# Modulation vectors turned in pairs by transposes, an early first split, and a factor applied after the last output tile of mixer two

## What is computed

```python
mod = (silu(c) @ w_ada[l] + b_ada[l])          # 6 x 1024
shift_m, scale_m, gate_m, shift_f, scale_f, gate_f = split(mod, 6)
h = rms_norm(x, norm_mix[l]) * (1 + scale_m) + shift_m
x = x + gate_m * hybrid_mixer(h, ...)          # stick-breaking heads and gated linear attention
h = rms_norm(x, norm_ffn[l]) * (1 + scale_f) + shift_f
x = x + gate_f * hierarchical_moe(h, ...)      # 32 experts
...
# layers of the second kind
mix = concat([rms_norm(y_a, g_a), y_b, rms_norm(y_c, g_c), rms_norm(y_d, g_d)])
x = x + mix @ w_out[l]
x = x + square(relu(rms_norm(x, g) @ w_up[l])) @ w_down[l]
```

## Time and profile before

| | us |
|---|---|
| median of three runs | 1703.4 (1702.81 to 1707.79) |
| profiled execution, its own time | 1698.64 |
| its span | 1696.8 |
| TensorE busy | 1616.9 |
| VectorE busy | 1175.3 |
| ScalarE busy | 927.8 |

### The profile page before, as it was taken

The page is one execution under the profiler, slowest core; times in us unless marked ns, Lnnn a source line. Parts: engine busy times, 40 slices in busy tenths (PEclk is TensorE's granted clock), DMA queues, the critical chain, the costliest instruction groups (busy, mean ns, idle before and its releaser), DMA issues.

```text
span 1696.8 us, 24960 instructions
## 1 busy us (share of the span) xinstructions
PE 1616.9 (95%) x10392; PEld 1385.3 (82%) x10392; DVE 1175.3 (69%) x1380; ACT 927.8 (55%) x1192; POOL 99.1 (6%) x68
## 2 busy tenths in 40 slices
PE   6999989999999999899999998998999999989997
PEld 3676779999996687699999987777999886879996
DVE  2644578999997635879999987685545586755554
ACT  3361457777776442477777765365444454544442
POOL 0200000101010200000110101100000011000000
PEclk9999999999999999999999999999999999989999
DMA  9768728999996766259999995052665532435551
GB/s 329 281 228 297 261 77 337 349 370 346 374 346 226 253 213 248 99 194 373 347 361 358 350 348 132 19 198 91 205 203 184 168 93 99 150 100 195 181 195 63
DMA packets 132534, 392.12 MB, mean 231 GB/s; under 512 B 23360, under 2 KB 36672, under 8 KB 107840
## 3 DMA queue, kind: packets, MB, share of 16 engines
q1 hardware_dynamic: 131840, 388.35, 64.5%
q10 hardware_dynamic: 576, 2.10, 0.4%
HBM read 389.37 MB, written 1.05 MB: 230 GB/s over the span
## 4 chain that ended last, share of the span: by engine, by line
PE 86%; DVE 6%; ACT 3%; POOL 2%; DMA 1%; issue 1%; SPq 0%; POOLq 0%; ACTq 0%; DVEq 0%
PE ps L1169 19%; PE ps L473 12%; PE ps L2150 10%; PE ps L1194 9%; PE ps L453 5%; PE ps L1648 4%; PE ps L1672 3%; PE ps L516 2%; PE ps L641 2%; PE ps L532 2%; PE ps L1624 2%; PE ps L1693 2%; PE ps L1708 1%; POOL hh L1409 1%; DVE spl L369 1%
## 5 line engine op out<-in xcount | busy, mean ns | idle before, releaser
L369 DVE TENSOR_TENSOR spl<-ring,spl 128x2048 fp32r<-128x2048 f32 x255 | 592.3, 2325 | 184.2 <-ACT spl L360 183.9
L360 ACT ACTIVATE spl<-ring 128x2048 fp32r<-128x2048 f32 x254 | 486.8, 1917 | 179.0 <-PE ps L473 107.7
L1169 PE MATMUL ps<-spl,ur 128*128 128x256 f32 x3072 | 370.7, 280 | 1.2 <-DVE ur L1392 1.2
L1169 PEld LDWEIGHTS ps<-spl,ur 128*128 128x128 f32 x3072 | 359.3, 190 | 2.4 <-DVE ur L1392 2.0
L473 PEld LDWEIGHTS ps<-hh,spl 128*128 128x128 f32 x1728 | 205.2, 190 | 7.7 <-issue 5.9
L473 PE MATMUL ps<-hh,spl 128*128 128x256 f32 x1728 | 207.4, 281 | 2.8 <-DVE hh L436 2.8
L1194 PE MATMUL ps<-spl,hh 128*128 128x512 f32 x768 | 186.6, 392 | 2.1 <-DVE hh L1363 2.1
L2150 PE MATMUL ps<-spl,ur 128*128 128x512 f32 x768 | 176.7, 389 | 0.0
L815 DVE TENSOR_TENSOR spl<-ring,spl 128x1024 fp32r<-128x1024 f32 (+2 forms) x126 | 144.9, 1176 | 37.9 <-ACT spl L806 37.0
L806 ACT ACTIVATE spl<-ring 128x1024 fp32r<-128x1024 f32 (+2 forms) x128 | 124.4, 1016 | 78.7 <-PE ps L453 23.9
L2150 PEld LDWEIGHTS ps<-spl,ur 128*128 128x128 f32 x768 | 143.2, 188 | 29.2
(11 more groups left out here) (360 smaller groups left out, 1746.1 us busy)
## 6 DMA issues: line engine op xcount, KB each, us to landing
ring<-in_w_up SPq DMA_DIRECT2D x96, 1024.0 KB, 5.3
ring<-in_w_down SPq DMA_DIRECT2D x96, 1024.0 KB, 5.1
ring<-in_w_gate SPq DMA_DIRECT2D x64, 1024.0 KB, 5.0
ring<-in_w_ada SPq DMA_DIRECT2D x48, 1024.0 KB, 7.1
ring<-in_w_in SPq DMA_DIRECT2D x34, 1024.0 KB, 7.7
ring<-in_w_out SPq DMA_DIRECT2D x16, 1024.0 KB, 7.7
ring<-in_w_in SPq DMA_DIRECT2D x8, 384.0 KB, 3.4
gate<-in_b_ada ACTq DMA_DIRECT2D x4, 512.0 KB, 5.7
```

The costliest lines, as they stand in the source:

```text
L360: sc.activation(t.hi, t.raw, ACT.Copy).then_inc(s_hi, 2)
L369: v.tensor_tensor(t.lo, t.raw, t.hi, ALU.subtract).then_inc(s_lo, 1)
L1169: ins = pe.matmul(ps[:, 2 + e % 2, 256 * z:256 * z + 256], le, ri, start=(k == 0 and j == 0 and z == 0), stop=(k == 7 and j == 2), skip_gr ...
```

## The change

- **Pairs.** Two vector blocks are summed one after the other in the same bank and copied into the two halves of a buffer. Then eight transposes (`pe_ada_turn`) with a permuted identity turn them; each writes 128 columns, four from each of which hold the four partial sums, the others zeros that the next transpose overwrites. VectorE reduces the four and adds the bias for all 128 partitions at once. There are 8 pairs; the two at the start take the place of four moves, and none stands ahead of the row transposes. The pair buffer of the lanes is the storage of the FFN gate, so its bias is loaded later, by SyncE ahead of the first output tile, behind a wait for the last pair before block 10. Layer 1's blocks 0 to 3 now come before layer 0's blocks 10 and 11.
- **Start.** VectorE forms the rest of the first tile in two halves, one before and one after the first pair of staged rows. The 16-column projection L680 comes after three projection steps instead of before them. Five dummy matmuls follow the second turn.
- **Orders.** The strings of mixer one are written anew; the chunks of the projection keep their sequence (`IN1`), with the waits for free banks in a function.
- **Flag.** It is read earlier: by TensorE in the slots of expert 0, by the other two at expert 16.
- **Mixer two.** Branch D is transposed without its factor; its output tile goes to banks of its own (`OD`), VectorE adds the first three tiles to `x` and then the last one times the factor. Two dummy matmuls stand behind D's transposes and two ahead of the first mixer two.

```diff
+IN1 = (0, 1, 2, 3, 4, 5)
...
-            blocks = [(l, c) for c in range(4, 12)] + [(1, c) for c in range(4) if l == 0]
+            blocks = [(l, c) for c in range(4, 10)] + [(1, c) for c in range(4) if l == 0] + [(l, 10), (l, 11)]
...
-        ev = [carve(16384, 512)] + [carve(512 * q, 512) for q in range(4)]
+        ev = [carve(16384, 512), carve(0, 2, 512), carve(1024, 2, 512), gate[:, 1, :].rearrange("p (c n) -> p c n", n=512)]
...
+        spread = ident.rearrange("p (j r) -> p r j", r=32)
+
+        def pe_ada_turn(pe, l, c, bank, e):
+
+            pe.wait_ge(s_ev, ada_copies(l, c))
+            for k in range(8):
+                ins = pe.transpose(ps[:, bank, 4 * k:4 * k + 128].rearrange("p (r j) -> p r j", j=4), e[:, :, k::8], spread)
+            ins.then_inc(s_adp, 1)
...
+            v.wait_ge(*own_dve(v.tensor_reduce(o, ps[:, bank, 0:32].rearrange("p (k j) -> p k j", j=4), AX.X, ALU.add)))
+            ins = v.tensor_tensor(o, o, PR(f"bm{l}")[:, 8 * s:8 * s + 8], ALU.add)
...
                 run(pe_ada_sum(pe, 0, 0, 4))
                 run(pe_ada_sum(pe, 0, 1, 5))
                 pe.wait_ge(s_ld, 32)
-                pe_ada_move(pe, 0, 0, 4, ev[1])
...
             if l == 0:
                 run(pe_ada_sum(pe, 0, 2, 6))
-                pe_ada_move(pe, 0, 1, 5, ev[2])
+                pe_ada_turn(pe, 0, 0, 4, ev[1])
                 run(pe_ada_sum(pe, 0, 3, 7))
-                pe_ada_move(pe, 0, 2, 6, ev[3])
-                pe_ada_move(pe, 0, 3, 7, ev[4])
+                pe_ada_turn(pe, 0, 2, 6, ev[2])
+                pe_spin(pe, 5, 5, cst[:, 0:C_HOT])
...
                 yield from pe_ada_sum(pe, al, c, 7)
-                pe_ada_move(pe, al, c, 7, ev[0])
+                if not ada_pair(al, c):
+                    pe_ada_gate(pe, al, c)
+                    yield
+                    continue
+                pe.wait_ge(s_ev, ada_copies(al, c) - 1)
+                yield from pe_ada_sum(pe, al, c + 1, 7)
+                pe_ada_turn(pe, al, c, 7, ev[3])
...
+            if l == 0:
+                pe.wait_ge(s_used, T["in", 0, IN1[0], 0].m + 1)
...
+        def dve_first(v, q):
+
+            t = splits[0]
+            h = halves(t)[q]
+            v.wait_ge(s_hi, 2)
+            ins = v.tensor_tensor(t.lo[:, h], t.raw[:, h], t.hi[:, h], ALU.subtract)
...
-            for q, s in ((0, 2), (1, 5)):
-                sc.dma_start(gate[:, q, :], a["b_ada"][l, s * 1024:(s + 1) * 1024].partition_broadcast(128)).then_inc(s_gb, 16)
+            sc.dma_start(gate[:, 0, :], a["b_ada"][l, 2048:3072].partition_broadcast(128)).then_inc(s_gb, 16)
...
+                for l in range(2):
+                    if t is T["out", l, 0]:
+                        sy.wait_ge(s_adp, ada_n[l, 10])
+                        sy.dma_start(gate[:, 1, :], a["b_ada"][l, 5120:6144].partition_broadcast(128)).then_inc(s_gf, 16)
...
+                if k == 7:
+                    pe.wait_ge(s_flag, l + 1)
+                    over = pe.value_load(flags[0:1, l, 0:1], min_val=0, max_val=1)
...
-        OB = (0, 1, 2, 6)
+        OB, OD = (0, 1, 2, 6), (3, 4, 5, 7)
...
-            yield from pe_fin2(pe, l, "D", V + 19)
+            yield from pe_fin2(pe, l, "D", None)
...
+            if br == "D":
+                pe_spin(pe, 3, 2)
...
             pe_x_T(pe, 4 + 2 * l)
+            if l == 0:
+                pe_spin(pe, 6, 2)
...
+            v.wait_ge(s_used, T["out2", l, 2].m + 1)
+            for c in range(2):
+                for i in range(2):
+                    xs = x[:, i, 512 * c:512 * c + 512]
+                    ins = v.tensor_tensor(xs, xs, ps[:, OB[2 * c + i], :], ALU.add)
+            v.wait_ge(*own_dve(ins))
+            v.wait_ge(a_ms, 13 * l + 13)
...
-                    dve_add(v, c, i, ps[:, OB[2 * c + i], :], None)
+                    xs = x[:, i, 512 * c:512 * c + 512]
+                    v.scalar_tensor_tensor(xs, ps[:, OD[2 * c + i], :], st[:, 208 + i:209 + i], xs, ALU.mult, ALU.add).then_inc(s_x, 1)
```

More of the change, by code:

```diff
@@ L506, in dve_cond, with ada_pair, ada_copies @@
             v.tensor_copy(cr[:, 1, :], C("mneg"))
-        ev = [carve(16384, 512)] + [carve(512 * q, 512) for q in range(4)]
-        ada_n = {(l, c): n for n, (l, c) in enumerate([(0, c) for c in range(12)] + [(1, c) for c in range(12)])}
+        ev = [carve(16384, 512), carve(0, 2, 512), carve(1024, 2, 512), gate[:, 1, :].rearrange("p (c n) -> p c n", n=512)]
+        PAIRS = [(0, 0), (0, 2)]
+        for _l in range(2):
+            PAIRS += [(_l, 4), (_l, 5), (_l, 6), (_l, 8)] + [(1, 0), (1, 2)] * (_l == 0) + [(_l, 10), (_l, 11)]
+        ada_n = {p: n for n, p in enumerate(PAIRS)}
+        def ada_pair(l, c):
+            return c // 2 not in (2, 5)
+        def ada_copies(l, c):
+            return sum(1 + ada_pair(*p) for p in PAIRS[:ada_n[l, c] + 1])
         def pe_ada_sum(pe, l, c, bank):
@@ L523, in act_ada, with pe_ada_gate @@
             sc.activation(e, ps[:, bank, :], ACT.Copy).then_inc(s_ev, 1)
-        def pe_ada_move(pe, l, c, bank, e):
-            s, h = divmod(c, 2)
-            pe.wait_ge(s_ev, ada_n[l, c] + 1)
-            if s in (2, 5):
-                ins = pe.matmul(ps[:, bank, :], C("ones"), e, start=True, stop=True)
-            else:
-                for k in range(8):
-                    ins = pe.matmul(ps[64 * h:64 * h + 64, bank, k:k + 1], e[:, k::8], C("ones")[:, 0:1], start=True, stop=True)
-            ins.then_inc(s_adp, 1)
+        def pe_ada_gate(pe, l, c):
+            pe.wait_ge(s_ev, ada_copies(l, c))
+            pe.matmul(ps[:, 7, :], C("ones"), ev[0], start=True, stop=True).then_inc(s_adp, 1)
@@ L552, in dve_ada @@
             ins.then_inc(s_adf, 1)
         def ada_blocks(l):
-            return [(l, c) for c in range(4, 12)] + ([(1, c) for c in range(4)] if l == 0 else [])
+            return [p for p in PAIRS[2:] if (p[0] == l and p[1] > 3) or (l == 0 and p[1] < 4)]
         m1 = Mem()
@@ L837, in act_ada_lane @@
             for al, c in ada_blocks(l):
-                act_ada(sc, al, c, 7, ev[0])
-                yield
+                if not ada_pair(al, c):
+                    act_ada(sc, al, c, 7, ev[0])
+                    yield
+                    continue
+                for h in range(2):
+                    act_ada(sc, al, c + h, 7, ev[3][:, h, :])
+                    yield
         def act_gla(sc, l):
@@ L900, in dve_mix1 @@
             if l == 0:
-                for c in range(4):
+                for c in (0, 2):
                     dve_ada(v, 0, c, 4 + c)
+                dve_first(v, 0)
             for k2 in range(4):
@@ L951, in dve_ada_lane @@
             for al, c in ada_blocks(l):
+                if not ada_pair(al, c):
+                    dve_ada_gate(v, al, c)
+                    yield
+                    continue
                 dve_ada(v, al, c, 7)
@@ L1155, in pe_moe @@
             pe_spin(pe, 4, 3)
[L1156 removed]
+            pe_rest(pe, l, over)
             for n in (0, 2):
@@ L1869, in act_fin2, with act_factor2 @@
         def act_fin2(sc, l, br, turned):
+            if br != "D":
+                act_factor2(sc, l, br)
+                yield
+            act_turned2(sc, l, br, turned)
+            yield
+            if br == "D":
+                act_factor2(sc, l, br)
+                yield
+        def act_factor2(sc, l, br):
             c0 = BR[br][2]
```

155 lines of the change are left out of this document (82 added, 73 removed), and 6 rows, old and new, of the table ORDER.

## The result

The changed kernel takes **1673.45 us** (median of four runs, 1673.37 to 1674.22) against 1703.69 us for the kernel before on the same chip: ratio 0.982, 95% interval 0.980 to 0.984. Forecast were 1673 us, 1661 to 1689, and 0.93 for faster. So far the number. The large terms came with their signs, but the sum promised 5 us more than the two profiled executions show, and the agreement with the median to 0.5 us is partly chance, as follows.

A forecast was written before the change was run, and what follows sets the result against it. TensorE was taken to bound mixer one, and latency the end of mixer two. Terms summed to -30.3 us, from 1698.64 to 1668.3 for a profiled execution; with 4.8 for the median, 1673 was forecast, range 1661 to 1689.

The forecast's parts named there:

- Moves, -16.8: Modulation after the start: twelve one-column moves of 2.0 us replaced by six pairs at 1.2 us; bounds -18.0 and -11.4.
- The upper bound (2.1): Modulation turns: at most 2.1 us per pair, if the strided identity costs 140 ns more per transpose, as L1162's weights do.
- Clock, -3.0: Stretches behind one-column moves (L532): three dips of 1.5 us each mostly go with the moves; bounds 0 and -4.5 us.
- transposes do not hold the clock: Rival, behind the six turns: 1.5 us lost after each and old dips stay, 1685 us; chance 0.08.
- The start, -4.7: Start of layer 0: L453 begins at 36.5 us, all done at 51.5 against 56.2; bounds -2.7 and -6.5 us.
- cost nothing: Start: five warming matmuls lie in the gap from 31 to 35 us and add no time.
- Gate bias, +1.3: Layer 1's mixer one: the later bias lands 2 to 3 us behind the gate's matmul, VectorE stands; bounds 0 and +3.
- First output tile, +2.6: Layer 0's mixer one: new order leaves 6.7 us of TensorE work from tile issue to use, before 7.8; bounds 0, +3.8.
- Mixer two, -9.2: Last output tile, both layers: shorter wait gives -5.6 us, held clock -1.4 and -2.2; bounds -5.6 and -9.2.
- Small ones: Early flag read: 0, bounds -1.5 and +1.5 us; two dummies ahead of mixer two: -0.5 us.
- the stage is TensorE's alone: Mixer one: removed TensorE work shortens it one for one; the rival denying this gives 1685 us, chance 0.11.
- an out-projection that ends 18 us earlier: Sign for mixer one: layer 0's out-projection ends some 18 us earlier, layer 1's some 24 to 26 us earlier.

The follow-up runs named there:

- packed kernel: Changed kernel with turns reading the identity packed and writing the bank with a step of 16 bytes: 1667.42 us, ratio 0.9799; repeated 1667.43 us, ratio 0.9807.
- the moves of 3.8 us: Changed kernel with each pair moved by eight one-column matmuls instead of transposes, VectorE's reduction removed: 1701.75 us, ratio 1.0003.
- the six of 1.8 us: Pairs moved by one-column matmuls, with the stationary columns side by side instead of 8 apart (output in wrong places): 1678.58 us, one run.
- the repeat's profile: Profile of the changed kernel run once more, unaltered: median 1676.35 us, ratio 0.9833 to the kernel before.
- the second comparison: Changed kernel again, unaltered, timed beside the kernel before: 1676.35 against 1702.82 us, ratio 0.9833.
- the one profile with them: Changed kernel with one dummy matmul ahead of layer 0's third state product and two ahead of its first output tile: 1676.72 us, ratio 0.9833.

## Why the prediction was right, term by term

**Moves, -16.8: -13.8 by the rows.** Twelve moves of 1.9 to 2.0 us went, as counted. A turn costs 1.61 to 1.91 us and not 1.2: six are 10.2 us instead of 7.2. The term was mis-sized by 3.0 us. I had the two right rows before me, L411's free step and L1162's dear one, and took the step of a *stationary* operand in a transpose as the nearer witness for a *moving* one. The packed kernel shows the difference, 0.075 us per transpose. The upper bound (2.1) held. By the Trainium skill (SBUF — State Buffer, the note on cachelines under its port tables), read as I did in the prediction, this term would stand at its upper bound; the runs lie between that and my value. For the moving operand and for a float32 matmul's weights the runs agree with it (0.20 against 0.125 us, 334 against 192 ns), for a transpose's weights they don't.

**Clock, -3.0: -4.4 for the old dips, and a new one of +3.1.** L474 behind a turn takes 3.09 us where 4.50 stood, likewise at the second dip: -2.9. In layer 0 the old dip went (1.5) and a larger one of 3.1 us came behind the wait at L733. What I gave as the reason, a move that hardly streams, is borne out in part: behind the moves of 3.8 us all six have a dip, behind the twelve of 2.0 us in the kernel before three, behind the six of 1.8 us none. The dips that the rival "transposes do not hold the clock" foresaw did not come: full speed behind every turn. That is not to say that transposes hold it, since one-column moves as short as the turns had no dip either. The Trainium skill (TensorE: Matmul & The Clock Gate, Part 4), by which transposes don't count as busy, would have had dips there; turns of 1 to 2 us between other matmuls show none here.

**The start, -4.7: -3.7.** The timeline that answers to the earlier trace rows:

```profile
37.54 8.49 PE L454 MATMUL ps<-spl,hh 128*128 128x512 f32 x36 [1.11 <-DVE spl L928]
45.96 3.63 PE L702 MATMUL ps<-ar,ring 128*16 128x256 f32 x16
49.52 3.01 PE L454 MATMUL ps<-spl,hh 128*128 128x512 f32 x12
```

The 48th ends at 52.46 (forecast 51.5). The one us is the landing of the first projection tile, which I had at 31.0. ScalarE waits for it until 32.11, and staging (L804) follows the split of that tile. It is not the dearer turn. With the packed identity the turn ends 1.4 us sooner, but staging starts only 0.5 us sooner, by as much as the tile lands sooner. The changed kernel, then the packed one:

```profile
32.11 1.91 ACT L361 ACTIVATE spl<-ring 128x2048 fp32r<-128x2048 f32 x1 [1.02 <-DMA ring<-in_w_in]
...
33.93 3.73 ACT L804 ACTIVATE ar<-ps,aff 128x256 f32<-128x256 f32 x8
```

```profile
31.63 1.91 ACT L361 ACTIVATE spl<-ring 128x2048 fp32r<-128x2048 f32 x1 [1.01 <-DMA ring<-in_w_in]
...
33.44 3.73 ACT L804 ACTIVATE ar<-ps,aff 128x256 f32<-128x256 f32 x8
```

The dummies were to "cost nothing" and are worth 1.6 us. No run takes back the early split or the later L680, so the share of each in the -3.7 is not shown.

**Gate bias, +1.3: 0.** VectorE does stand for it in layer 1, as I wrote:

```profile
645.37 0.69 DVE L556 TENSOR_TENSOR gate<-gate,ps 128x512 f32<-128x512 f32 x1 [4.39 <-DMA gate<-in_b_ada]
```

But nothing of it reaches TensorE, whose waits in layer 1's mixer one are the same as before, each to 0.1 us.

**First output tile, +2.6: right in size (the wait went from 0.83 to 2.65 us, +1.8), wrong in mechanism.** I took it for the tile's landing; it is the order on ScalarE and VectorE, and the wait grew since the 6.0 us from the end of the last projection step to the start of the wait became 3.7.

**Mixer two, -9.2: -9.7.** 4.4 us in layer 0 and 5.2 in layer 1. In other shares than written: the wait ahead of the transposes fell by 2.3, not 2.8, the last tile follows them 0.5 us sooner, and the clock gives 4.1 us, of which 3.0 hang on the two dummies in each layer.

**Small ones.** The 0.9 us wait for VectorE behind layer 1's experts is gone in the profile of the changed kernel (forecast 0, bounds 1.5). Five other profiles with the early read have it at 0.3 to 1.2 us, so the -0.9 below can't be put down to the flag. The dummies at mixer two's entry gained nothing at the entry, 6.45 us from L422 to L1699 as before.

**What no term had: +4.6.** The step that failed is "the stage is TensorE's alone", whose failure I gave as a rival with 0.11 and against which I held that the kernel before shows no wait for a tile there. That holds for the old order. The new one brought waits of 1.6 (L779), 1.5 (L733) and 0.8 us (L528, where 0.5 stood) and the dip of 3.1, less the wait of 1.9 at L663 that went. In the repeat's profile the same places come to +2.1, with 1.6 more for the dip at L655: how much this step costs changes with the dips. For the start and mixer one of layer 0 the rows give -3.7 for the start, -16 + 6.9 for eight moves and four turns, -1.5 for the old dip, +1.8 for the tile and +4.6: -7.9, where the table has -8.0. The forecast had some -14 there. Its own sign for this stage, an out-projection that ends 18 us earlier, was larger still, and so was that for layer 1, 24 to 26 us where the terms add up to some 21. They end 8.0 and 14.1 us earlier. The lower end of the range, written as 1661, comes to 1663 by its own terms.

All terms by the rows: -13.8 - 4.4 - 3.7 + 1.8 - 9.7 - 0.9 + 4.6 = -26.1 us. The spans differ by 25.2; the 0.9 left are not placed (mixer one of layer 1 should have given 7.6 and gave 6.7; the stages that nothing touched differ by up to 1.3 either way). My sum promised 5 us more than the spans gave. The medians differ by 30.2 since the kernel before loses more to its clock in most executions than in the profiled one; in the second comparison they differ by 26.5.

## What to carry to other kernels

When an order written out by hand is new, read the old trace for chains whose links on another engine take longer than the gaps that the new order leaves them: "no wait here" holds for the old order alone. Before a term is priced by a row, ask whether that row steps the same operand of the same kind of instruction. And set a sum made against one profiled execution against that execution; if it meets the median instead, that is no confirmation.

## What the runs showed of the hardware

- A step in an operand costs by what the instruction does with it: in float32 transposes a stationary operand with a step of 32 bytes nothing (192 ns), in float32 matmuls of 128 columns 142 ns per load (334 against 192); a moving identity read with a step of 128 bytes 0.075 us per transpose (0.20 against 0.125). Writing the bank with a step of 16 bytes costs nothing that shows.
- One and the same wait is followed by the lower clock level in one execution and not in another (changed kernel, 2.65 us ahead of L655: the next 12 take 3.01 us and 4.57). Whether dummies in that gap help is not shown by the one profile with them. In the last tile of mixer two it is: with two dummies in the 2.56 us from the start of D's transposes to that tile, the next 24 matmuls take 5.7 us in every profile that has them, without them 7.1 and 7.3 in the one that was taken, and the tile starts no later.
- Executions of one kernel spread over some 8 us (changed kernel: 1671.8 to 1680.1). Profiles differ by such dips (144.7 and 150.4 us for mixer two of layer 1) and by a stall of 0 to 4.2 us behind layer 1's experts, which no row explains. What ends it stays open.
